# The state-space branch first: its projection leads, its steps stand between units of the attention projection, its lift stands ahead of attention

## The chip, the cores and the metric

The kernel runs on one core of one Trainium2 chip. The metric is the device time of one execution in microseconds (us). TensorE is called PE in the profile, VectorE DVE, ScalarE ACT, GpSimd POOL, and SP is the engine that issues most of the DMA transfers.

## The reference

It is one inference step of a small trunk with DEPTH = 2 layers over T = 384 tokens (three tiles of 128: one of context, two of latent tokens), D_MODEL = 1024, all in float32. Cut to what matters, a layer is:

```python
shift1, scale1, gate1, shift2, scale2, gate2 = mod      # six vectors from silu(c) @ w_ada + b_ada
h = rmsnorm(x) * (1 + scale1) + shift1
a, b, c, d, gate = split(h @ w_in)
ya = dense_attention(rope(norm(a_q)), rope(norm(a_k)) + cache, a_v + cache)        # branch A
yb = window_attention(..., sink)                                                   # branch B
yc = ssd_mixer(c_z, c_xbc, c_dt, state)                                            # branch C, state space
yd = rmsnorm(diff_attention(...)) * (1 - lam_init)                                 # branch D
out = sum(sigmoid(gate[n]) * (y[n] @ w_br[n]) for n in branches) @ w_out
x = x + gate1 * out
h2 = rmsnorm(x) * (1 + scale2) + shift2
x = x + gate2 * experts(h2)                              # 16 experts, each takes its own best tokens

def ssd_mixer(z, xbc, dt_raw, h0):                       # both directions
    u = silu(conv5(xbc)); xs, B, C = split(u)
    dt = softplus(dt_raw + bias); la = -exp(a_log) * dt
    acs = cumsum(la)                                     # per tile of 128 tokens
    y = ((C B^T) * exp(acs_i - acs_j)) (xs*dt) + C h_in * exp(acs) + d_skip * xs
    h_next = exp(acs_end) * h_in + B^T (to_end * xs*dt)
    return rmsnorm(y * silu(z))
```

## The kernel before

There is no planner. Each of the five engines has its instruction list written out by hand, once per layer (a hardware loop over li), and semaphores join them. What orders the work around the change is this.

**The banks.** Most products of TensorE go through four PSUM banks in turn. `big_results` (L82) writes down their order and which engine takes each. `bank(name)` (L596) makes TensorE wait until the result four places earlier has been taken; `grab` and `gave` are the other side. An engine takes its results in the order of its own list, so a result can be held up by something unrelated ahead of it there. Banks 4 to 7 belong to the attention steps and to the SSD products.

**The weights.** SP loads the 32 weight pieces of the mixers in the order of the numbers AT_ADA to AT_LIFT (L29 to L32) into a ring of SLOTS = 4 slots. Piece j goes to slot j % 4, and its transfer is issued only when TensorE has freed the slot from piece j - 4. A piece of w_ada, of a gate or of w_out has half the rows of a 1024x1024 block, 2 MB; a lift is one piece of 1 MB. Every product of two halves needs pieces j and j + 1.

**TensorE's order in a layer.** rows(0), rows(1) (products of the conditioning vector with w_ada), columns(0), columns(1) (their transposition); transposes of x (`widths`); projections of A and B (six units, 3 tiles x 2), of D (dqk and dv by tile), of C (z by tile, xbc by group of channels); six units of gate 0 with transposes of A's and B's queries and keys (qkT) among them, then the cached keys (ckT), D's (dT, cdT). Then the attention loop: for i = 0, 1, 2 (branches A, B, D) 12 steps (h, t) in a pipeline of scores, weights (transposes of the probabilities) and weighted, and in each step half a unit of gate(i + 1). After i = 0 and i = 1 stands lift(i): transposes of the branch (boT), then six products with w_br (up), which VectorE merges into xn. BRANCH = (0, 1, 3, 2), so C is last. rows(2) stands at the end of i = 2.

**The state-space part** stands behind all of this: transposes of the convolved channels (uT), the running sums (cum), the initial state (h0T), rows(3), decays(0), lift(2) for D, then for each tile t the scores GT, decays(t + 1) and, behind a wait for the masked scores (`mt_ready`, given by L1742), the products with Mt, xdt and xde. Then rows(4), the carried terms yo, columns(3), lift(3) for C, columns(4). The transposes of the merged m (mT) wait for `merged` at 18. Behind them stand the gate rows (gb), the output projection (out), rows(5) and the router, and then the expert stage.

**The other engines.** VectorE does the head norms with rotary embedding (`head_norm`, first A and B, then D), then the convolution (L1588, L1590), then the steps of attention, then the SSD elementwise work (L1694 to L1785, with C's norm at L1780). ScalarE copies results out of the banks, squares for the norms, takes the roots (`root(n)`, which waits for VectorE's variance), exp, silu and the tanh of the gates (L1237). The lines 578 and 587 are the helpers through which all of TensorE's matmuls and transposes go, so groups are told apart by tiles and shapes. Every float32 product shows as two passes in the profile.

Of the kernel before, what the change touches and what calls it, by code (L numbers as in the profile page):

```python
# [13 lines left out]
P = 128  # L14
D = 1024
# [23 lines left out]
BRANCH = (0, 1, 3, 2)  # L39
# [42 lines left out]
def big_results():  # L82
# [6 lines left out]
    out += [(("ab", t, b), "act") for b in range(2) for t in range(NT)]  # L89
    for t in range(NT):  # L90
        out += [(("dqk", t), "act"), (("dv", t), "act")]
    out += [(("z", t), "act") for t in range(NT)]
    out += [(("xbc", g), "act") for g in range(4)]
    out += [(("g", 0, s // 2, s % 2), "act") for s in range(3)]
    for t in range(NT):
        out += [(("qkT", t, b), "act") for b in range(2)] + [(("g", 0, (t + 3) // 2, (t + 3) % 2), "act")]
    out += [(("ckT",), "act")] + [(("dT", t), "act") for t in range(NT)] + [(("cdT",), "act")]
    for i in range(4):
        if i < 3:
            out += [(("g", i + 1, t, h), "act") for t in range(NT) for h in range(2)]  # L100
        if i == 2:
            out += [(("row", 2, h), "act") for h in range(2)]
            out += [(("uT", t), "act") for t in range(NT)]
            out += [(("cum",), "dve"), (("h0T",), "act")]
            out += [(("row", 3, h), "act") for h in range(2)]
            out += [(("dec", 0, d), "act") for d in range(2)]
        if i == 3:
            for t in range(NT):
                out += [(("GT", t, 0), "dve"), (("GT", t, 1), "dve")]
                if t + 1 < NT:  # L110
                    out += [(("dec", t + 1, d), "act") for d in range(2)]
            out.append((("row", 4, 0), "act"))
            out += [(("yo", t, g), "dve") for t in (1, 2) for g in range(2)]
            out += [(("row", 4, 1), "act"), (("col", 3), "dve")]
        out += [(("boT", i, k), "dve") for k in range(2)]
        out += [(("up", i, t, h), "dve") for t in range(NT) for h in range(2)]
    out.append((("col", 4), "dve"))
# [23 lines left out]
def trunk_kernel(nc, x_prompt, x_sample, cvecT, rowp, colp, caches, b_ada, w_ada, w_in, w_br, w_out, w_router,  # L141
                 w_e1, w_e3, w_e2, consts, y_prompt, y_sample, o_ak, o_av, o_bk, o_bv, o_ssm, o_dk, o_dv):
    with ExitStack() as ctx:
# [63 lines left out]
        cacc = at(po, 4 * NU_CONV).rearrange("p (i n) -> p i n", i=4)  # L207

        so = [qko]

        def over(n):
            so[0] += n
            assert so[0] <= qkend
            return at(so[0] - n, n)

        xsB = over(NT * 384).rearrange("p (t n) -> p t n", t=NT)
        E = over(8 * P).rearrange("p (j l) -> p j l", j=8)
        Mt = over(8 * P).rearrange("p (j l) -> p j l", j=8)
        xdt = over(1024).rearrange("p (i d h n) -> p i d h n", i=2, d=2, h=4)
# [100 lines left out]
        kv_out = sem("kv_out")  # L320
        ssm_out = sem("ssm_out")
# [182 lines left out]
        def _(pool):  # L504
            def parameters(li, first=False):
                pool.dma_start(cp[:, :], colp[li, :, :]).then_inc(params_c, 16)
                if first:

                    pool.wait_ge(loaded[(AT_AB + 1) % SLOTS], 16 * ((AT_AB + 1) // SLOTS + 1))
                    pool.dma_start(cst[:, NCST0:NCST], consts[:, NCST0:NCST]).then_inc(in_cst, 16)  # L510
# [10 lines left out]
            def mixers(li):  # L521
                pool.memset(xbc[:, :, :], 0.0).then_inc(pads, 1)

                pool.wait_ge(ab_ready, 1)
# [5 lines left out]
                pool.wait_ge(d_ready, 1)  # L530
                pool.dma_start(o_dk[0, li].rearrange("s h m d -> s (h m d)"), DQ[:, 0, 256:512]).then_inc(kv_out, 16)
                pool.wait_ge(big_act, taken_by(("dv", 0))[1])
                pool.dma_start(o_dv[0, li].rearrange("s h d -> s (h d)"), vd[:, 0, :]).then_inc(kv_out, 16)
# [7 lines left out]

                pool.wait_ge(st0_taken, 1)
                for d in range(2):
                    for g in range(2):
                        pool.dma_start(o_ssm[0, li, d, 2 * g:2 * g + 2].rearrange("h p n -> (h p) n"),
                                       sst[:, 2 * d + g, :]).then_inc(ssm_out, 16)
                bias_row(1, 5)
                pool.wait_ge(kv_out, (li + 1) * 96)
# [24 lines left out]
        def _(pe):  # L573
# [37 lines left out]
            with pe.Fori(0, DEPTH) as li:  # L611
# [73 lines left out]
                need(AT_AB)  # L685
                need(AT_AB + 1)
                for br in range(2):
                    for t in range(NT):
                        tokens(bank(("ab", t, br))[:, :], t, AT_AB, slice(br * 512, br * 512 + 512), signal=big,
                               free=(br == 1 and t == NT - 1))  # L690
                need(AT_D)
                need(AT_D + 1)
                for t in range(NT):

                    tokens(bank(("dqk", t))[:, :], t, AT_D, slice(0, 512), signal=big)
                    tokens(bank(("dv", t))[:, 0:ND_ - 512], t, AT_D, slice(512, ND_), signal=big, free=t == NT - 1)
# [14 lines left out]
                owed.append(freed[(AT_C + 1) % SLOTS])  # L711

# [17 lines left out]
                for s in range(3):  # L730
                    gate0(s)


                pe.wait_ge(in_cst, 16)
                pe.wait_ge(params, (li + 1) * 48)
                pe.wait_ge(ab_ready, 1)
                for t in range(NT):
                    for br in range(2):
                        b = bank(("qkT", t, br))
                        for g in range(2):  # L740
                            turn(b[:, g * P:(g + 1) * P], AB[:, t, br, g * P:(g + 1) * P])
                        turn(b[:, 256:384], AB[:, t, br, 256:384], signal=big)
                    gate0(3 + t)
                b = bank(("ckT",))
                turn(b[:, 0:P], ch("ak"))
                turn(b[:, P:2 * P], ch("bk"), signal=big)
# [7 lines left out]
                turn(b[:, P:2 * P], ch("dk")[:, P:2 * P], signal=big)  # L754
                taken(("cdT",))

# [69 lines left out]
                def lift(i):  # L826
                    j = AT_LIFT[i]
                    if i < 2:
                        pe.wait_ge(o_ready, (i + 1) * NIT)
                    else:  # L830
                        pe.wait_ge(bo_ready, i - 1)
                    for c in range(2):
                        b = bank(("boT", i, c))
                        for t in range(NT):
                            turn(b[:, t * P:(t + 1) * P], bo[:, t, c * P:(c + 1) * P], signal=big if t == NT - 1 else None)
# [10 lines left out]
                scores(0, 0)  # L846
                for i in range(3):
# [16 lines left out]
                pe.wait_ge(conv_out, 4)  # L864
                for t in range(NT):
                    b = bank(("uT", t))
                    for g in range(3):
                        turn(b[:, g * P:(g + 1) * P], uT[:, g, t * P:(t + 1) * P], signal=big if g == 2 else None)

                pe.wait_ge(dt_done, 1)  # L870
                b = bank(("cum",))
                for t in range(NT):
                    o = t * 16
                    mm(b[:, o:o + 4], c_("upto"), la[:, t, 0:4])
                    mm(b[:, o + 4:o + 8], c_("from"), la[:, t, 4:8])
                    mm(b[:, o + 8:o + 16], c_("ones"), la[:, t, :], signal=big if t == NT - 1 else None)
                b = bank(("h0T",))
                for d in range(2):
                    turn(b[:, d * P:(d + 1) * P], ch("ssm")[:, d * P:(d + 1) * P], signal=big if d else None)
                for h in range(2):  # L880
                    rows(3, h)

                def tri(d):
                    return c_("upto") if d == 0 else c_("from")


                def decays(t):
                    for d in range(2):
                        b = bank(("dec", t, d))
                        for h in range(4):  # L890
                            mm(b[:, h * P:(h + 1) * P], la[:, t, 4 * d + h:4 * d + h + 1].broadcast_to([P, P]), tri(d),
                               start=h == 0, stop=False, skip_group_check=True)
                        mm(b[:, :], ident, rep(c_("negbelow" if d == 0 else "negabove"), 1, 4), start=False, stop=True,
                           signal=big, skip_group_check=True)

                decays(0)
                lift(2)
                taken(("uT", 2))
                for t in range(NT):
                    for g in range(2):  # L900
                        b = bank(("GT", t, g))
                        r = slice(g * HD, (g + 1) * HD)
                        mm(b[:, 0:P], uT[r, 2, t * P:(t + 1) * P], uT[r, 3, t * P:(t + 1) * P], signal=big)
                    if t + 1 < NT:
                        decays(t + 1)
# [1083 lines left out]
```

## Time and profile before

| what | value |
|---|---|
| time, median of 3 runs | 2061.29 us (2060.68 to 2061.43) |
| the profiled execution, its own time | 2063.47 us |
| its span, first to last instruction | 2061.3 us |
| PE busy | 1910.1 us, 93% of the span |
| DVE, ACT, POOL busy | 481.8, 356.2, 48.2 us |
| mean granted TensorE clock | 0.965 of full speed |
| DMA | 532.98 MB, mean 259 GB/s |

The span falls into mixers and experts, twice. The mixers of layer 0 reach from 41.9 us (first projection) to 493.2 us (start of the output projection) and further to the first expert at 576 us; layer 1 repeats this from 1062 us on. PE busy is not PE at its peak, and the clock that was granted has to be read beside it.

### The profile page before, as it was taken

How to read it: one execution, taken by the hardware profiler on the slowest of the kernel's cores; microseconds unless marked ns; L12 is line 12 of the kernel's file. 1: busy time of each engine (PE TensorE's matmuls, PEld its weight loads, DVE VectorE, ACT ScalarE, POOL GpSimd, SP SyncE). 2: the span in 40 equal slices, each digit the busy share in tenths (PEclk: the TensorE clock that was granted, in tenths of full speed). 3: DMA queues.
4: the chain of work that ended last, by engine and by line, in shares of the span. 5: the costliest groups of instructions: out<-in, count | busy, mean ns of one | idle time of the engine just before them, and what ended most of it. 6: DMA issues, size and time to landing. Idle time of an engine off the chain costs nothing. (4 is left out here: it accounts for less than half of the span.)

```text
span 2061.3 us, 19828 instructions
## 1 busy us (share of the span) xinstructions
PE 1910.1 (93%) x7810; PEld 882.6 (43%) x7810; DVE 481.8 (23%) x1254; ACT 356.2 (17%) x920; POOL 48.2 (2%) x88
## 2 busy tenths in 40 slices
PE   5999999999899999898879999999998999989987
PEld 2464444455443433333345544544555333334322
DVE  1033124453410100100120522253534001001002
ACT  2123222421210100100021231224113001001000
POOL 2100000000300000000000000000000000000000
PEclk8999999988899999999989999999898999999999
DMA  9141113244689999999951411134436899999996
GB/s 376 62 166 68 52 51 123 90 183 179 227 327 408 426 429 428 428 429 428 422 207 62 174 61 62 41 123 171 159 122 245 351 426 424 429 428 428 429 428 271
DMA packets 65413, 532.98 MB, mean 259 GB/s; under 512 B 6657, under 2 KB 6785, under 8 KB 41281
## 3 DMA queue, kind: packets, MB, share of 16 engines
q1 hardware_dynamic: 62256, 527.59, 62.5%
q0 software_dynamic: 3088, 4.47, 0.6%
q8 instruction: 44, 0.72, 0.1%
q14 instruction: 25, 0.20, 0.0%
HBM read 529.16 MB, written 2.88 MB: 258 GB/s over the span
## 5 line engine op out<-in xcount | busy, mean ns | idle before, releaser
L578 PE MATMUL bank<-ring,hT 128*128 128x512 f32 (+2 forms) x1440 | 598.5, 569 | 2.7 <-DVE hT L1472 2.7
L578 PE MATMUL bank<-ring,scr 128*64 128x512 f32 (+1 forms) x2176 | 528.9, 598 | 44.4 <-DMA ring<-in_w_e 27.0
L578 PE MATMUL bank<-scr 128*64 128x512 f32 (+6 forms) x2048 | 437.7, 520 | 7.9 <-DVE dsm L1742 4.7
L578 PEld LDWEIGHTS bank<-ring,hT 128*128 128x128 f32 x1440 | 268.7, 191 | 271.3 <-issue 265.2
L578 PEld LDWEIGHTS bank<-ring,scr 128*64 128x64 f32 (+1 forms) x2176 | 175.6, 142 | 368.6 <-issue 309.1
L578 PEld LDWEIGHTS bank<-scr 128*64 128x64 f32 (+3 forms) x2048 | 183.2, 164 | 260.3 <-issue 251.9
L1885 DVE TENSOR_TENSOR scr<-scr,bank 128x512 f32<-128x512 f32 x32 | 22.0, 687 | 641.7 <-ACT scr L1394 641.7
L587 PE MATMUL bank<-cst,scr 128*128 128x128 f32 (+1 forms) x530 | 94.5, 294 | 40.4 <-ACT scr L1396 24.9
L587 PEld LDWEIGHTS bank<-cst,scr 128*128 128x128 f32 (+1 forms) x530 | 63.0, 159 | 102.3 <-issue 76.1
L1394 ACT ACTIVATE scr<-bank 128x512 f32<-128x512 f32 x32 | 19.1, 597 | 481.7 <-PE bank L578 481.7
L578 PE MATMUL bank<-ring,csw 128*32 128x512 f32 x384 | 58.0, 747 | 31.7 <-DMA ring<-in_w_ada 19.4
L1629 DVE TENSOR_REDUCE st<-bank 128x1 f32<-128x384 f32 (+1 forms) x48 | 22.5, 469 | 200.7 <-PE bank L578 200.6
L1398 ACT ACTIVATE scr<-bank 128x512 f32<-128x512 f32 x32 | 19.1, 597 | 247.3 <-PE bank L578 247.3
L578 PE MATMUL bank<-scr,xn 128*128 128x192 f32 (+3 forms) x288 | 50.5, 335 | 4.8 <-DVE scr L1850 2.4
L1237 ACT ACTIVATE scr<-bank 128x512 f32<-128x512 f32 x48 | 28.6, 597 | 138.3 <-PE bank L578 138.3
L578 PEld LDWEIGHTS bank<-scr,xn 128*128 128x128 f32 x288 | 44.8, 220 | 9.2 <-ACT scr L1389 5.1
L1286 ACT ACTIVATE scr<-bank,st 128x384 f32<-128x384 f32 (+1 forms) x48 | 24.5, 510 | 136.4 <-DVE st L1637 81.7
L1887 DVE COPY scr<-bank 128x384 f32<-128x384 f32 x32 | 17.9, 558 | 107.1 <-PE bank L587 107.1
L578 PE MATMUL bank<-hT,ring 128*128 128x384 f32 x128 | 41.6, 486 | 0.0
L578 PEld LDWEIGHTS bank<-ring,csw 128*32 128x32 f32 x384 | 12.7, 129 | 67.2 <-issue 43.0
L1292 ACT ACTIVATE scr<-bank,st 128x384 f32<-128x384 f32 (+1 forms) x48 | 24.0, 505 | 76.5 <-DVE st L1639 76.5
L1396 ACT ACTIVATE scr<-bank 128x512 f32<-128x512 f32 x32 | 19.1, 597 | 88.6 <-PE bank L587 88.6
(210 smaller groups left out, 1074.8 us busy)
## 6 DMA issues: line engine op xcount, KB each, us to landing
ring<-in_w_e SPq DMA_DIRECT2D x124, 2048.0 KB, 19.0
scr<-in_w_e SPq DMA_DIRECT2D x64, 2048.0 KB, 17.8
ring<-in_w_ada SPq DMA_DIRECT2D x24, 2048.0 KB, 9.9
ring<-in_w_in SPq DMA_DIRECT2D x20, 2048.0 KB, 8.0
ring<-in_w_br SPq DMA_DIRECT2D x8, 1024.0 KB, 7.2
ring<-in_w_out SPq DMA_DIRECT2D x4, 2048.0 KB, 8.6
ring<-in_w_in SPq DMA_DIRECT2D x4, 1552.0 KB, 16.3
ring<-in_w_in SPq DMA_DIRECT2D x4, 1536.0 KB, 6.7
```

Source lines behind the costliest of these rows:

```text
L578: ins = pe.matmul(out, lhsT, rhs, start=start, stop=stop, **kw)
L587: ins = pe.transpose(out, in_, ident[0:k, 0:k])
L1237: gave(("g", i, t, h), A(G[i % 2][:, t, h * HALF:(h + 1) * HALF], b[:, :], ACT.Tanh, scale=0.5))
L1286: ins = A(pr[:, n % 2, 0:nk], banks[4 + n % 2][:, 0:nk], ACT.Exp, bias=st[:, 1, q:q + 1], scale=HD ** -0.5, accum_out=st[:, 2, q:q + 1])
L1292: ins = A(pr[:, n % 2, m * T:m * T + nk], banks[4 + m][:, 0:nk], ACT.Exp, bias=st[:, 1, q + m:q + m + 1], scale=32 ** -0.5, accum_out=st[: ...
L1394: A(hs, banks[6][:, :], ACT.Silu).then_inc(silu_ready, 1)
L1396: A(hidT[:, :, :], banks[6][:, :].rearrange("p (b n) -> p b n", b=4), ACT.Copy).then_inc(hts_ready, 1)
L1398: A(yo, banks[7][:, :], ACT.Copy).then_inc(yo_ready, 1)
L1629: link(V.tensor_reduce(mx[:, 0:1], banks[4 + n % 2][:, 0:nk], AX.X, ALU.max))
L1885: V.tensor_tensor(hid.rearrange("p n b -> p (n b)"), hs, banks[7][:, :], ALU.mult).then_inc(hid_ready, 1)
L1887: V.tensor_copy(sgT.rearrange("p t c -> p (t c)"), banks[6][:, 0:T]).then_inc(sgs_ready, 1)
```

## The change

The order of branches is C, A, B, D. C is projected first (z, xbc), then D's dqk; dv stands behind the transposes uT. cum and h0T follow. The six units of the A/B projection alternate with decays, scores and products of the SSD steps; the carried terms follow the last unit. Of gate 0 two units stand ahead of the transposes of D and of the cached keys, three between them and the transposes of A's and B's queries and keys, one behind these. lift(0), now C's, stands between the first scores and the attention loop; lift(1) and lift(2) (A, B) stand where lift(0) and lift(1) stood, and lift(3) is D's. rows(3), rows(4), columns(3) and columns(4) follow the loop directly, ahead of lift(3). On VectorE the convolution, the SSD steps and C's norm move ahead of the head norm of A and B. On ScalarE C's squares and root(3) stand between two tanhs, and the squares of A and B and root(36) ahead of the evictions of D's transposes. E has two buffers; E, Mt and xdt lie in xn, the rest in the second gate buffer; C's result has a buffer of its own (boC). POOL stores D's keys and values and the final states ahead of A's and B's.

```diff
-AT_ADA = (0, 2, 20, 22, 25, 30)
-AT_AB, AT_D, AT_C, AT_OUT = 4, 6, 8, 28
-AT_GATE = (10, 12, 15, 18)
-AT_LIFT = (14, 17, 24, 27)
+AT_ADA = (0, 2, 21, 23, 25, 30)
+AT_C, AT_D, AT_AB, AT_OUT = 4, 6, 8, 28
+AT_GATE = (10, 13, 16, 19)
+AT_LIFT = (12, 15, 18, 27)
-BRANCH = (0, 1, 3, 2)
+BRANCH = (2, 0, 1, 3)
+AB_UNITS = [(t, b) for b in range(2) for t in range(NT)]
...
     out += [(("z", t), "act") for t in range(NT)]
     out += [(("xbc", g), "act") for g in range(4)]
+    out += [(("dqk", t), "act") for t in range(NT)]
+    out += [(("uT", t), "act") for t in range(NT)]
+    out += [(("dv", t), "act") for t in range(NT)]
+    out += [(("cum",), "dve"), (("h0T",), "act")]
...
+    out += [(("yo", t, g), "dve") for t in (1, 2) for g in range(2)]
+    out += [(("g", 0, s // 2, s % 2), "act") for s in range(2)]
+    out += [(("dT", t), "act") for t in range(NT)] + [(("cdT",), "act"), (("ckT",), "act")]
+    out += [(("g", 0, s // 2, s % 2), "act") for s in range(2, 5)]
+    out += [(("qkT", t, b), "act") for t in range(NT) for b in range(2)]
+    out += [(("g", 0, 2, 1), "act")]
...
         if i == 3:
+            out += [(("row", v, h), "act") for v in (2, 3, 4) for h in range(2)]
+            out += [(("col", 3), "dve"), (("col", 4), "dve")]
...
@@ TensorE @@
+                ab_unit(0)
+                decays(0)
+                ab_unit(1)
+                state_scores(0)
+                decays(1)
+                ab_unit(2)
+                state_products(0)
+                state_scores(1)
+                decays(2)
+                ab_unit(3)
+                state_products(1)
+                state_scores(2)
+                ab_unit(4)
+                state_products(2)
+                ab_unit(5)
+                pe.wait_ge(h_in, 1)
+                carried(1)
+                carried(2)
...
                 scores(0, 0)
+                lift(0)
                 for i in range(3):
...
                     if i < 2:
                         scores(i + 1, 0)
-                        lift(i)
+                        lift(i + 1)
+                for v in (3, 4):
+                    for h in range(2):
+                        rows(v, h)
                 columns(3)
+                columns(4)
                 lift(3)
-                columns(4)
...
@@ ScalarE @@
+                gate(0, 0)
+                for t in range(NT):
+                    act.wait_ge(u_ready, t + 1)
+                    A(Mt.rearrange("p j l -> p (j l)")[:, 256 * t:256 * (t + 1)], boC[:, t, :], ACT.Square,
+                      accum_out=st[:, 5, t:t + 1]).then_inc(act_sq, 1)
+                root(NT)
+                gate(0, 1)
+                act.wait_ge(d_ready, 1)
+                act.wait_ge(big_act, taken_by(("ab", NT - 1, 1))[1])
+                for t in range(NT):
+                    if t >= 2:
+                        act.wait_ge(sq_free, NT + t - 1)
+                    A(tmp[:, t % 2, :], AB[:, t, :, :].rearrange("p b n -> p (b n)"), ACT.Square).then_inc(act_sq, 1)
+                root(36)
+                for t in range(NT):
+                    b = grab(("dT", t))
+                    if t == 0:
+                        act.wait_ge(mt_ready, 2)
+                    A(dqT[:, :, t * P:(t + 1) * P], b[:, 0:256].rearrange("p (g t) -> p g t", g=2), ACT.Copy)
+                    gave(("dT", t), A(dkT[:, :, t * P:(t + 1) * P], b[:, 256:512].rearrange("p (g t) -> p g t", g=2), ACT.Copy))
```

## Rows read from the trace of the kernel before

**Rows 1.** Busy time by stretch, expert stage of layer 0: engines, granted clock, DMA share, GB/s

```profile
600.00:1000.00 400.00, 374.53 (x1751) 139.27 (x1748) 39.71 (x100) 32.35 (x59) 0.00 (x0) 1.00 1.00 423
```

**Rows 2.** Waits of TensorE, 40 to 495 us: releaser, us in total, times, longest

```profile
...
PE bank L578 <- DVE dsm L1742: 2.3, 1, 2.3
PE bank L587 <- DVE scr L1780: 2.2, 1, 2.2
...
PE bank L578 <- ACT scr L1265: 1.1, 1, 1.1
PE bank L587 <- ACT scr L1286: 0.6, 1, 0.6
PE bank L578 <- issue: 0.6, 1, 0.6
```

**Rows 3.** Timeline of TensorE, layer 0: start, us, operation, passes, wait before

```profile
188.83 1.47 PE L587 MATMUL bank<-cst,scr 128*128 128x128 f32 x12
...
406.20 1.92 PE L578 MATMUL bank<-ring,csw 128*32 128x512 f32 x16
...
412.07 5.05 PE L578 MATMUL bank<-ring,csw 128*32 128x512 f32 x32 [0.63 <-issue]
...
459.60 3.89 PE L578 MATMUL bank<-cst,scr 128*128 128x2 f32 x16
...
467.85 13.11 PE L578 MATMUL bank<-ring,scr 128*128 128x512 f32 x24 [0.65 <-DVE scr L1603]
480.79 3.66 PE L578 MATMUL bank<-cst,scr 128*128 128x2 f32 x16
484.32 5.36 PE L587 MATMUL bank<-cst,xn 128*128 128x128 f32 x24
...
539.89 3.23 PE L587 MATMUL bank<-cst,xn 128*128 128x128 f32 x24 [1.75 <-DVE xn L1462]
```

**Rows 4.** Busy time by stretch, at the lower clock: columns as in rows 1

```profile
483.20:490.50 7.30, 7.30 (x32) 6.80 (x33) 2.58 (x6) 1.96 (x4) 0.00 (x0) 0.53 1.05 436
462.90:473.10 10.20, 7.39 (x16) 3.86 (x17) 4.68 (x13) 0.38 (x2) 0.00 (x0) 0.50 0.79 321
449.40:456.00 6.60, 6.60 (x34) 4.09 (x32) 1.77 (x6) 0.00 (x0) 0.00 (x0) 0.51 0.00 0
411.80:415.00 3.20, 2.93 (x16) 0.91 (x20) 1.55 (x6) 0.12 (x1) 0.00 (x0) 0.50 1.03 413
193.40:196.70 3.30, 3.25 (x5) 1.63 (x6) 0.22 (x2) 0.84 (x3) 0.00 (x0) 0.53 0.72 297
```

**Rows 5.** Timeline of ScalarE: squares of A and B; tanh; a copy of dT

```profile
83.96 1.58 ACT L1195 ACTIVATE scr<-scr 128x768 f32<-128x768 f32 x2
...
188.81 0.60 ACT L1237 ACTIVATE scr<-bank 128x512 f32<-128x512 f32 x1 [1.89 <-PE bank L578]
...
189.84 0.40 ACT L1263 ACTIVATE scr<-bank 128x256 f32<-128x256 f32 x1
```

**Rows 6.** Timeline of VectorE: variance of A and B; SSD step 1

```profile
87.75 0.18 DVE L1443 TENSOR_SCALAR st<-st 128x36 f32<-128x36 f32 x1
...
439.79 0.42 DVE L1758 TENSOR_TENSOR scr<-scr,bank 128x256 f32<-128x256 f32 x1 [3.22 <-PE bank L578]
440.25 0.69 DVE L1716 TENSOR_TENSOR scr<-scr 128x512 f32<-128x512 f32 x1
440.86 1.28 DVE L1738 TENSOR_TENSOR scr<-scr,bank 128x512 f32<-128x512 f32 x2
```

**Rows 7.** Two loads of w_ada on SP's queue, each with its landing

```profile
L414 SPq DMA_DIRECT2D ring<-in_w_ada x1: 367/367/367, 404.6 to 404.6; - x1
...
DMA to landing us min/median/max: 7.4/7.4/7.4
...
L414 SPq DMA_DIRECT2D ring<-in_w_ada x1: 367/367/367, 416.3 to 416.3; - x1
...
DMA to landing us min/median/max: 9.9/9.9/9.9
```

More of the change, by code:

```diff
@@ L540, in mixers @@
                 bias_row(0, 2)
[L542 to L546, printed above, removed]
                 bias_row(1, 5)
-                pool.wait_ge(kv_out, (li + 1) * 96)
+                pool.wait_ge(kv_out, (li + 1) * 64)
+                pool.sem_inc(dummy, 1)
+                pool.wait_ge(d_out, (li + 1) * 32)
                 pool.sem_inc(dummy, 1)
@@ new lines, in _ @@
+                for t in range(NT):
+                    tokens(bank(("dv", t))[:, 0:ND_ - 512], t, AT_D, slice(512, ND_), signal=big, free=t == NT - 1)
+                pe.wait_ge(dt_done, 1)
+                b = bank(("cum",))
+                for t in range(NT):
+                    o = t * 16
+                    mm(b[:, o:o + 4], c_("upto"), la[:, t, 0:4])
+                    mm(b[:, o + 4:o + 8], c_("from"), la[:, t, 4:8])
+                    mm(b[:, o + 8:o + 16], c_("ones"), la[:, t, :], signal=big if t == NT - 1 else None)
@@ new lines, in _, with ab_unit @@
+                b = bank(("h0T",))
+                for d in range(2):
+                    turn(b[:, d * P:(d + 1) * P], ch("ssm")[:, d * P:(d + 1) * P], signal=big if d else None)
+                def ab_unit(n):
+                    t, br = AB_UNITS[n]
+                    if n == 0:
+                        need(AT_AB)
+                        need(AT_AB + 1)
+                    tokens(bank(("ab", t, br))[:, :], t, AT_AB, slice(br * 512, br * 512 + 512), signal=big,
+                           free=n == len(AB_UNITS) - 1)
@@ new lines, in tri, with decays @@
+                def tri(d):
+                    return c_("upto") if d == 0 else c_("from")
+                def decays(t):
+                    for d in range(2):
+                        b = bank(("dec", t, d))
+                        for h in range(4):
+                            mm(b[:, h * P:(h + 1) * P], la[:, t, 4 * d + h:4 * d + h + 1].broadcast_to([P, P]), tri(d),
+                               start=h == 0, stop=False, skip_group_check=True)
+                        mm(b[:, :], ident, rep(c_("negbelow" if d == 0 else "negabove"), 1, 4), start=False, stop=True,
+                           signal=big, skip_group_check=True)
@@ L728, in gate0 @@
                         gate(0, s, part)
[L730 to L746, printed above, removed]
+                gate0(0)
+                gate0(1)
                 pe.wait_ge(d_ready, 1)
@@ L877, in _ @@
[L877 to L894, printed above, removed]
@@ new lines, in decay @@
+                def decay(t):
+                    if t == 2:
+                        act.wait_ge(mt_ready, 1)
+                    for d in range(2):
+                        b = grab(("dec", t, d))
+                        for h in range(4):
+                            ins = A(E[t % 2][:, 4 * d + h, :], b[:, h * P:(h + 1) * P], ACT.Exp,
+                                    bias=nacs[:, t, 4 * d + h:4 * d + h + 1])
+                        gave(("dec", t, d), ins)
+                root(48)
+                ab_unit(0)
@@ new lines, in _ @@
+                sqs[0] += NT
+                dve.wait_ge(act_sq, sqs[0])
+                dve.wait_ge(u_ready, NT)
+                y = rsqrt(st[:, 5, 0:NT], NT, 256)
+                for t in range(NT):
+                    ins = V.scalar_tensor_tensor(boC[:, t, :], boC[:, t, :], y[:, t:t + 1], r_("gssm"), ALU.mult, ALU.mult)
+                    if t == NT - 1:
+                        ins.then_inc(bo_ready, 1)
+                    else:
+                        step(ins)
+                settle()
@@ L1775, in _ @@
[L1775 to L1785 removed]
+                        lift(i + 1)
```

557 lines of the change are left out of this document (260 added, 297 removed).

## The prediction

> **What bounds the kernel now.** I read the busy times by stretch first. In the expert stage the DMA engines are full, 423 GB/s from 600 to 1000 us [rows 1]; that stream starts on the progress of TensorE behind the mixers, so the stage keeps its length and only shifts. The mixers are the other way round. From 41.9 us (first projection of layer 0) to 493.2 us (first output projection) TensorE almost never stops; the waits that it has, apart from those of the lifts and of the step to branch D, which both kernels have, are in [rows 2], a few us a layer. Everything that the diff touches lies in this stretch, once per layer, so the price is: work of TensorE + its waits + what it loses to a lower clock, times two.
>
> The work is the same in both: the same matmuls and transposes, in another order. So I compare losses. The timeline [rows 3] and the granted clock [rows 4] show the second kind: in five stretches of 3.2 to 10.2 us the clock is at 0.50 to 0.55, the lower of the two levels (1.2 GHz for 2.4), and half of such a stretch is lost. Times below are those of layer 0.
>
> **What the change takes away, per layer.**
> - a. The entry to attention: waits of 1.1 and 0.6 us for the last transposed keys and the first exp [rows 2], then 3.3 us at half clock [rows 4]. The lift of C now stands there and covers them: 1.7 + 1.65 = 3.4.
> - b. The wait of 0.6 before rows(3) [rows 2] and 3.2 us at half clock [rows 4]: 0.6 + 1.6 = 2.2. (Its successor is g.)
> - c. The wait of 2.3 for Mt in the third SSD step [rows 2] and 6.6 us at half clock [rows 4]: 2.3 + 3.3 = 5.6. In the new place units of the A/B projection, 16 passes of 512 columns each, stand between the steps.
> - d. The wait of 2.2 for C's norm (L1780) [rows 2]: 2.2. C's norm is now needed only after six gate units.
> - e. columns(4), 16 passes 2 columns wide, moves from behind lift(3) to ahead of it. The transposes of m then come after a lift at full clock: 24 of them take 5.36 now, 3.23 in the same form later [rows 3]: 2.1.
>
> Sum 15.5 us.
>
> **What it adds, per layer.**
> - f. A wait at the cached-key transposes. ScalarE's order is now gate(0,1), three squares of AB, root(36), and only then the evictions of dT. The bank of ckT is that of dT 0, four results earlier. After the gate unit ends, ScalarE needs 0.6 for the tanh, then squares and VectorE's sums take from 83.96 to 87.93, 4.0 [rows 5, 6], then the root and two copies of 0.4 that overlap [rows 5], some 0.9: 5.5. TensorE has only 12 transposes, 1.47 [rows 3], and two more, 1.7 in all. It waits 3.8, and 0.2 for the next bank. Behind the waiting instruction stand gate units 2 to 4, which would have been ready. A clock loss like a's follows: 4.0 + 1.65 = 5.7. Bounds: 4.0 to 7.4.
> - g. rows(3) needs the second half of its weights, whose slot is freed by the last gate unit of the loop, which ends at 403.5. Its place in the queue is that of the load issued at 404.6 with 7.4 to landing: 412.0 [rows 7]. Now four us of state-space work (transposes, cum, h0T) stand between rows(2), which ends at 408.1 [rows 3], and rows(3); they are gone. Wait 4.0 plus b's clock loss of 1.6: 5.6. Bounds 4.0 to 7.4.
> - h. rows(4) follows at once, where SSD steps and a lift now give its loads more than 20 us. Its two loads wait for slots that rows(2) frees, are issued some 4 and 5 us after 403.5, and stand in the queue behind g's: 4.19 MB more. At 413 GB/s [rows 4] that is 10.2 us behind 412.0; by the landing at 426.2 of the load issued at 416.3, when 5.24 MB had followed in 14.2 us [rows 7], it is 11.4. I take 422.7. rows(3) runs from 412.0 for 5.1 [rows 3], to 417.1. Wait 5.6 plus clock 1.6: 7.2. Bounds 5.0 to 9.6.
> - i. The transposes of m wait for the last merge: two VectorE operations over 512 columns (L1616, L1618), 0.69 each like that at 440.25 [rows 6], 1.6 with latency. Today columns(4), 3.66 [rows 3], covers this. 1.6 (bounds 1.4 to 3.2).
> - j. The two columns stand back to back, 7.5 us with almost no columns streamed; the clock falls in them. The one measured partly at half clock took 3.89 beside 3.66 [rows 3]. 0.6 (0 to 2). lift(3) runs partly at half clock in both: 13.1 for 24 passes [rows 3].
>
> Sum 20.7 us. The nine transposes, cum (3 us of small passes, 0 to 1.6 of clock) and the SSD in front I put at nothing: what covers them is the projection. The load order costs nothing elsewhere, since use and queue have the same order in both; projecting C first (1.5 MB halves instead of 2) only makes the first weights earlier, and VectorE's hT, not the load, releases TensorE there. The stores of o_ssm and o_dk move forward on POOL's queue, are 32 to 128 KB, and no stage waits for them within tens of us.
>
> Net 20.7 - 15.5 = +5.2 per layer, +10.4 in two. The profiled span is 2061.3 (2063.5 with what lies around it), the median 2061.29, so the same base: **2071.7 us**.
>
> One rule of the Trainium skill differs from a row here. In "DMA: Bandwidth & Descriptors", section "Where 436 GB/s comes from", the HBM side binds a load at about 358 GB/s per core. The trace does not agree: 413 in the tail, 423 in the expert stage. By the rule h's loads would take 11.7 instead of some 10.7, 2 us more in two layers: 2073.7.
>
> **The rivals.**
> - R1, the columns do not drop the clock, so lift(3) runs at full speed. That saves half of 10.2 us less its idle part, some 3.3, and j: 3.9 a layer: 2071.7 - 7.8 = 2063.9, no measurable change. For it: at 412 to 473 each fall also had a real wait near. Against: from 483.2 to 490.5 TensorE was busy all of 7.30 us at 0.53 [rows 4], with only columns(4) ahead of it. The Trainium skill ("TensorE: Matmul & The Clock Gate", Part 1: The HAM clock gate) has the clock fall after an idle stretch, which here would mean R1; this last row speaks against that reading.
> - R2, the other side: g and h vanish, because the ada loads land ahead. Price 12.8 a layer: 2071.7 - 25.6 = 2046, faster. It decides from 7.2 of the 12.8 on. For it: DMA is idle through most of the attention. Against: four slots, and each load waits for the slot of four loads earlier, whose last reader is the last gate unit or rows(2) itself.
> - R3, the SSD steps stall in front too. Least slack: after the products of step 0 VectorE adds (0.42), decays (0.69) and multiplies (0.64, half of 1.28) [rows 6], 1.9 with latencies, before the bank of the next A/B unit is free. TensorE has 24 passes of scores and decays meanwhile, which take longer than the 3.23 of 24 transposes [rows 3]: over 1.3 of slack. The convolution and norm D have more. If this fails by 2 us in two steps, or by 2 us with a clock loss like a's, some 3.7 a layer: 2079.
> - R4, f does not come (5.7 a layer): 2060.3, the same. Nothing in the order of the program speaks for it.
>
> **How the numbers follow.** A measurement of this kernel tells some 0.2% from no change, 4.1 us. Forecast 0.50, R1 0.13, R2 0.12, R3 0.17, R4 0.08. Slower by over 0.2% (above 2065.4): the forecast nearly all (0.48) and R3: 0.65. Within: R1, R4, the rest of the forecast, less their spill: 0.20. Faster: R2 and spill: 0.15. The forecast's own bounds: all low ends give 14.4 - 15.5 = -1.1 a layer, 2059; all high ends, the 1.6 of cum with them, 31.2 - 15.5 = +15.7, 2093, but hardly all at once: 2064 to 2082. The range reaches down to take in R1 and R4 and leaves R2 out: 2058 to 2084.
>
> **What would show it.** In the profile after: no wait at Mt in the third step and no half clock near it (c); a wait of about 4 us for ScalarE's dT evictions ahead of the cached keys (f); waits of about 4 and 5.6 us on ring loads of in_w_ada in a place where none over 1 us is now (g, h); a wait of 1.6 on xn ahead of the transposes of m (i), whose 24 take 3.2; attention entered without a wait. Wrong would be: f's evictions early, rows(4) starting less than 14 us after the last gate unit, or waits between the A/B units.

## The result, and the profile of the changed kernel

The changed kernel takes 2069.2 us (median of 6 runs, 2067.3 to 2072.3) beside 2061.4 for the kernel before: a ratio of 1.0039, 95% interval 1.0026 to 1.0052. It is slower by some 8 us. One run of the kernel before took 2546 us, and the ratio leaves it out. The forecast of 2071.7 stands, and so does its sign.

Layer 0 of the profiled execution, span 2066.8 us. First the waits of TensorE from 40 to 500 us (releaser, us in total, times, longest); they answer to [rows 2].

```profile
PE bank L587 <- DMA ring<-in_w_ada: 9.0, 2, 4.9
PE bank L596 <- ACT scr L1319: 3.9, 1, 3.9
PE bank L587 <- DVE scr L1731: 3.5, 4, 1.1
PE bank L596 <- DVE scr L1791: 1.6, 1, 1.6
PE bank L596 <- DVE xn L1744: 1.5, 1, 1.5
...
```

The waits at Mt, for C's norm, at the entry to attention and before rows(3) are gone. In their place stand one for ScalarE's copies of dT (L1319), two for loads of w_ada and one for the last merge (L1744). The other two rows belong to both kernels. Now the timeline of TensorE that answers to [rows 3]:

```profile
183.22 0.38 PE L596 MATMUL bank<-cst,ca 128*128 128x128 f32 x2
187.52 0.44 PE L596 MATMUL bank<-cst,ca 128*128 128x128 f32 x2 [3.92 <-ACT scr L1319]
...
443.53 1.92 PE L587 MATMUL bank<-ring,csw 128*32 128x512 f32 x16
...
446.20 1.92 PE L587 MATMUL bank<-ring,csw 128*32 128x512 f32 x16
453.04 6.15 PE L587 MATMUL bank<-ring,csw 128*32 128x512 f32 x32 [4.91 <-DMA ring<-in_w_ada]
463.24 6.17 PE L587 MATMUL bank<-ring,csw 128*32 128x512 f32 x32 [4.05 <-DMA ring<-in_w_ada]
469.34 7.63 PE L587 MATMUL bank<-cst,scr 128*128 128x2 f32 x32
...
479.00 12.06 PE L587 MATMUL bank<-ring,scr 128*128 128x512 f32 x24 [0.65 <-DVE scr L1731]
492.57 2.84 PE L596 MATMUL bank<-cst,xn 128*128 128x128 f32 x24 [1.51 <-DVE xn L1744]
```

From 443.53 on: rows(2) in two halves, rows(3) behind a wait of 4.91, rows(4) behind one of 4.05 (it starts 19.7 us after the gate units end), both columns, lift(3), the transposes of m. And the stretches at the lower clock, columns as in [rows 4], with the whole mixers of the layer as the last row:

```profile
188.20:191.60 3.40, 3.40 (x5) 1.51 (x6) 3.33 (x5) 2.20 (x5) 0.00 (x0) 0.54 0.00 0
382.60:386.60 4.00, 3.63 (x6) 1.62 (x7) 2.56 (x8) 1.40 (x5) 0.00 (x0) 0.57 0.95 347
451.60:458.10 6.50, 5.06 (x24) 1.19 (x28) 0.00 (x0) 0.60 (x1) 0.00 (x0) 0.50 1.03 393
461.70:468.40 6.70, 5.16 (x28) 1.23 (x32) 0.00 (x0) 0.60 (x1) 0.00 (x0) 0.50 0.73 259
471.90:482.10 10.20, 9.55 (x32) 7.57 (x33) 1.64 (x5) 0.00 (x0) 0.00 (x0) 0.50 1.03 414
40.10:498.70 458.60, 438.90 (x1548) 228.39 (x1549) 152.42 (x406) 113.89 (x337) 19.45 (x35) 0.97 0.29 109
```

The mixers take 458.6 us. In the kernel before they took 451.3, with this row of its own:

```profile
41.90:493.20 451.30, 439.26 (x1547) 232.55 (x1548) 153.54 (x406) 112.82 (x336) 20.85 (x37) 0.97 0.30 115
```

The second number is TensorE's busy time: idle time went from 12.0 to 19.7, up 7.7; busy time hardly moved (439.3 to 438.9). So the layer paid in waits, and won next to nothing from the clock. Layer 1 says the same: its mixers went from 451.8 to 457.6.

### The profile page after: what moved, and what is told of

It is laid out like the page before. It is cut to its first block and busy times, and to the rows that moved or that the text cites. A ratio compares the mean times of both kernels' runs of the same rounds, so it can differ in the third digit from the quotient of the medians.

```text
span 2066.8 us, 19836 instructions
## 1 busy us (share of the span) xinstructions
PE 1902.0 (92%) x7810; PEld 868.5 (42%) x7810; DVE 480.5 (23%) x1254; ACT 359.5 (17%) x922; POOL 48.2 (2%) x88
## 5 line engine op out<-in xcount | busy, mean ns | idle before, releaser
L587 PE MATMUL bank<-scr 128*64 128x512 f32 (+7 forms) x1952 | 423.9, 530 | 0.9 <-ACT scr L1434 0.9
L587 PEld LDWEIGHTS bank<-scr 128*64 128x64 f32 (+3 forms) x1952 | 169.3, 160 | 254.8 <-issue 254.3
```

What stands on the lines that cost most here:

```text
L587: ins = pe.matmul(out, lhsT, rhs, start=start, stop=stop, **kw)
```

## The experiments

All are edits of the changed kernel, each timed beside the kernel before. Medians in us, ratio to the kernel before with its 95% interval:

| run | edit | median | ratio |
|---|---|---|---|
| x1 | copies of dT first on ScalarE | 2059.6 | 1.0002 (0.9989 to 1.0015) |
| x2 | lift(3) between rows(3) and rows(4) | 2054.2 | 0.9975 (0.9963 to 0.9987) |
| x3 | rows(2) ahead of lift(2) | 2059.5 | 1.0003 (0.9991 to 1.0016) |
| x4 | columns(4) behind lift(3) | 2067.6 | 1.0043 (1.0026 to 1.0060) |
| x5 | half of the bytes of rows(3), (4) left out | 2061.3 | 1.0004 (0.9994 to 1.0015) |
| x6 | SSD steps behind all A/B units | 2085.3 | 1.0125 (1.0105 to 1.0145) |
| x8 | x2 and x3 | 2051.0 | 0.9952 (0.9937 to 0.9967) |
| x7 | x1, x2 and x3 | 2036.0 | 0.9890 (0.9873 to 0.9908) |
| x9 | x7, columns inside the output projection | 2030.5 | 0.9851 (0.9835 to 0.9868) |
| x10 | only the columns inside the output projection | 2063.8 | 1.0012 (1.0000 to 1.0025) |
| x0 | none | 2074.0 | 1.0071 (1.0057 to 1.0085) |

The ratios tell each kernel from the kernel before. What an edit is worth beside the changed kernel is less sure: that kernel itself gave 1.0039 on one chip and 1.0071 on another, 7 us apart. So the times decide only where they differ by more, or where two runs share a chip (x1 to x4, x5 to x8, x10 and x0); the single steps are read from the traces.

**x1, step f.** On ScalarE:

```
 gate(0, 1)
 act.wait_ge(d_ready, 1)
+for t in range(NT):  # dT, then cdT and ckT
+    b = grab(("dT", t))
...
 for t in range(NT):
     A(tmp[:, t % 2, :], AB[:, t, :, :]..., ACT.Square)
 root(36)
-for t in range(NT):
-    b = grab(("dT", t))
...
```

> ScalarE evicts dT, cdT and ckT directly behind tanh(0,1), ahead of the squares and the root of the attention norm. Nothing else moves. Theory (step f of the prediction: the wait of 3.9 at ckT and the half clock of 3.4 us behind it come from the squares and the root standing in front of the evictions): both go, 5.6 us a layer, so 11 us in all and a time near 2058 us (2056 to 2061). Rival A: what is late is what the evictions need themselves, not their place; then they wait as long and the time stays at 2069. Rival B: squares and root now end some 2.5 us later and TensorE waits at qkT behind gate unit 4 instead; the wait moves, with 0 to 3 us a layer gained and a new row there.

TensorE's timeline of x1 at the cached keys:

```profile
185.11 0.60 PE L596 MATMUL bank<-cst,ca 128*128 128x128 f32 x4
185.76 20.87 PE L587 MATMUL bank<-ring,hT 128*128 128x512 f32 x48
```

The wait is gone, none replaces it at qkT, and TensorE runs on at full clock. The output projection starts 5.6 us sooner (493.07 for 498.68), although the first projection of this execution began 1.9 later (41.94 for 40.05): the mixers took 451.1 and 450.8, 7.5 and 6.8 less. That is more than f; in layer 0 the half clock at the D step, worth 1.7, is absent too. The order on ScalarE was the whole cause of the wait. What stood in front of the copies is seen in ScalarE's timeline of the changed kernel; a table load of 1.28 is part of it:

```profile
182.60 1.57 ACT L1312 ACTIVATE scr<-scr 128x768 f32<-128x768 f32 x2
184.53 0.84 ACT L1312 ACTIVATE scr<-scr 128x768 f32<-128x768 f32 x1 [0.36 <-DVE st L1517]
185.39 1.28 ACT L1171 ACT_TABLE_LOAD   x1
186.69 0.23 ACT L1171 ACTIVATE st<-st 128x36 f32<-128x36 f32 x1
186.82 0.37 ACT L1318 ACTIVATE scr<-bank 128x256 f32<-128x256 f32 x1
```

**x2, steps h, i and e.** On TensorE, and alike in the order of results and on the other engines:

```
-AT_ADA = (0, 2, 21, 23, 25, 30)
+AT_ADA = (0, 2, 21, 23, 26, 30)
-AT_LIFT = (12, 15, 18, 27)
+AT_LIFT = (12, 15, 18, 25)
...
 rows(3, h)
+lift(3)
 rows(4, h)
 columns(3)
 columns(4)
-lift(3)
```

> The state-space-independent lift(3) stands between rows(3) and rows(4), and columns(3) and (4) behind rows(4); the ring's order follows (lift piece 25, rows(4) pieces 26 and 27). Theory (step h: rows(4) waits because nothing but rows(3) lies between the end of the gate units and the landing of its second half; step i: mT waits for the last merge): both waits, 4.05 and 1.5, and the clock loss of 1.6 behind the first go; the two columns steps now stand right ahead of mT, whose 24 transposes fall back to half clock (2.8 to 5.4 us). Net 4.7 us a layer gained, near 2060 us (2056 to 2064). Rival A: the transfers are simply that long; the wait moves to lift(3)'s piece or to the output projection's pieces and little is gained (2066 to 2070). Rival B: columns do not lower the clock; mT keeps 2.8 and the time is near 2055.

Its timeline:

```profile
452.41 5.19 PE L587 MATMUL bank<-ring,csw 128*32 128x512 f32 x32 [4.55 <-DMA ring<-in_w_ada]
...
459.19 10.57 PE L587 MATMUL bank<-ring,scr 128*128 128x512 f32 x24 [0.79 <-DVE scr L1732]
469.69 3.64 PE L587 MATMUL bank<-ring,csw 128*32 128x512 f32 x32
473.26 7.63 PE L587 MATMUL bank<-cst,scr 128*128 128x2 f32 x32
480.75 5.36 PE L596 MATMUL bank<-cst,xn 128*128 128x128 f32 x24
```

rows(4) starts without a wait and takes 3.64 instead of 6.17; mT has no wait either, but takes 5.36. The stretches from lift(3) on, the columns from 473.3 to 480.9 in two parts:

```profile
459.20:473.30 14.10, 14.10 (x57) 5.46 (x57) 8.28 (x12) 0.60 (x1) 0.00 (x0) 1.00 0.98 375
473.30:476.10 2.80, 2.80 (x17) 2.80 (x13) 0.00 (x0) 0.60 (x1) 0.00 (x0) 0.99 1.02 392
476.20:480.90 4.70, 4.70 (x22) 4.70 (x22) 0.17 (x1) 0.00 (x0) 0.00 (x0) 0.50 1.02 417
480.90:486.00 5.10, 5.10 (x25) 5.10 (x26) 2.02 (x5) 1.96 (x4) 0.00 (x0) 0.50 1.03 413
```

TensorE is busy for all of the 12.7 us behind 473.3, and for 14.1 us ahead of them it had no wait at all; still the clock falls within the columns. That decides against R1: it falls without a wait while these matmuls, two columns wide, run. The time, 2054.2, is below the range that I gave (2056 to 2064) and is that of rival B, but rival B's sign, mT at 2.8, did not come. The mixers gained 10.8 and 7.6, not 4.7: the rest is clock, since rows(3), rows(4), lift(3) and its six transposes all ran shorter (5.19, 3.64, 10.57 and 0.87 for 6.15, 6.17, 12.06 and 1.52), and the half clock at the D step was absent in layer 0.

**x3, steps g and h.** rows(2) and its pieces ahead of lift(2):

```
-AT_ADA = (0, 2, 21, 23, 25, 30)
+AT_ADA = (0, 2, 18, 23, 25, 30)
-AT_GATE = (10, 13, 16, 19)
+AT_GATE = (10, 13, 16, 21)
-AT_LIFT = (12, 15, 18, 27)
+AT_LIFT = (12, 15, 20, 27)
...
 if i == 2 and n >= NIT:
-    rows(2, n - NIT)
+    rows(3, n - NIT)
 if i < 2:
     scores(i + 1, 0)
+    if i == 1:
+        for h in range(2):
+            rows(2, h)
     lift(i + 1)
```

> rows(2) and its two pieces stand ahead of lift(2), in the middle of attention; rows(3) takes its place in the last two gate slots, with pieces that are asked for long before. Rows(4), columns and lift(3) follow as in the changed kernel. Theory (steps g and h are one shortage: four pieces asked for in the last 20 us): the wait of 4.9 at rows(3) and its clock loss of 1.6 go; rows(4) still waits about 4 and loses 1.6, because its pieces are asked for only when the last gate units free their slots. 6.5 us a layer gained, near 2056 us (2053 to 2060). Rival A: the wait at rows(4) grows by what rows(3) loses, the sum stays, 2066 to 2070. Rival B: rows(2) in the middle waits itself for its pieces, or delays the first scores of the third branch, and 2 us or more of the gain are given back there.

One wait on w_ada is left (4.32 ahead of rows(4)); rows(2) brings none in the middle. The mixers took 452.6 and 451.5, 6.0 and 6.1 less, near the 6.5 expected. The median fell by less than the 13 us that two layers should give, but ended inside the range.

**x4, steps e and j.**

```
 columns(3)
-columns(4)
 lift(3)
+columns(4)
```

> columns(4) goes back behind lift(3), as in the kernel before; all else as changed. Theory (steps e, i, j): mT's wait of 1.5 for the last merge goes, since columns(4) covers it; mT stands right behind columns(4) at half clock again, 5.4 instead of 2.8 us; columns(3) alone is at full clock when it starts. Net +0 to +1 us a layer: 2068 to 2072. Rival (the columns do not lower the clock): mT keeps 2.8 and the wait goes, so 1.5 us a layer or more gained, near 2066.

```profile
484.87 3.66 PE L588 MATMUL bank<-cst,scr 128*128 128x2 f32 x16
488.39 4.27 PE L597 MATMUL bank<-cst,xn 128*128 128x128 f32 x24
```

mT's wait is gone and its 24 transposes take 4.27 instead of 2.84: i is taken away and e comes back, in part (5.4 was expected), and the median is 1.7 below the changed kernel's and just below the range given, too little to tell from it. The columns cost 3.89 and 3.66 apart and 7.63 together, so j is 0.1.

**x5, what g and h wait for.**

```
 for v in range(6):
-    plan[AT_ADA[v] + h] = (w_ada[li, rows, v * D:(v + 1) * D], D, 4)
+    n = HALF if v in (3, 4) else D
+    plan[AT_ADA[v] + h] = (w_ada[li, rows, v * D:v * D + n], n, 4)
...
-cols = slice(h * HALF, (h + 1) * HALF)
+cols = slice(0, HALF) if v in (3, 4) else slice(h * HALF, (h + 1) * HALF)
```

Half of these two weight matrices is left out; both halves of each product come from the same 512 columns.

> The pieces of rows(3) and rows(4) are loaded with 512 of their 1024 columns, and both halves of each are computed from these 512; so half of these two weight matrices is left out. The count of instructions on TensorE is the same. Theory (steps g and h: the waits are the bytes of four pieces at some 420 GB/s, asked for too late): the wait of 4.9 at rows(3) falls to 2 to 3, the one of 4.05 at rows(4) goes with its clock loss of 1.6. 8 us a layer, near 2053 us (2048 to 2060). Rival: a transfer's fixed time from issue to landing, not its bytes, makes the wait; then the waits stay within 1 us of 4.9 and 4.05, and the time stays above 2064.

```profile
452.83 3.64 PE L588 MATMUL bank<-ring,csw 128*32 128x512 f32 x32 [1.63 <-DMA ring<-in_w_ada]
459.12 3.64 PE L588 MATMUL bank<-ring,csw 128*32 128x512 f32 x32 [2.64 <-DMA ring<-in_w_ada]
```

With half the bytes the waits go from 4.91 and 4.05 to 1.63 and 2.64, and the clock no longer falls behind them: both rows take 3.64. So bytes make about half of the waits (9.0 to 4.3 in all). I had expected the second to vanish, and the time at 2053 (2048 to 2060); it came out at 2061.3, outside. Why the second stays is seen on SP's queue: the last load of rows(4) is issued at 453.9, only 1.1 us after rows(3) starts, and lands 5.2 later, when rows(4) starts (the section on the prediction says what holds its issue back). The mixers gained 9.1 and 7.2, about as reckoned. In the profiled execution the stretches outside the mixers took 9.5 us more than in that of the changed kernel; x0 below shows how far these move by themselves.

**x6, step c.** All six `ab_unit` ahead of the first `decays`, on TensorE, on ScalarE and in the order of results:

```
-ab_unit(0)
-decays(0)
-ab_unit(1)
...
+for n in range(len(AB_UNITS)):
+    ab_unit(n)
+decays(0)
+state_scores(0)
+decays(1)
+state_products(0)
...
```

> All six A/B units first and only then the three state-space steps, one behind the other, on TensorE and ScalarE alike; the rest as in the changed kernel. Theory (steps b and c: what took the waits at Mt and the half clock near them away is that the steps stand between A/B units): each step now waits for decay exponentials on ScalarE and for Mt on VectorE, with nothing to cover it. At least the 2.3 at Mt and half clock around it come back, 5 to 12 us a layer more, 2079 to 2093 us, near 2085. Rival: what took them away is only that the state-space branch comes before attention, wherever its steps stand; then no wait at Mt and 2067 to 2071 us.

```profile
PE bank L583 <- DVE dsm L1667: 2.3, 1, 2.3
...
PE bank L583 <- DVE dsm L1685: 0.8, 1, 0.8
```

```profile
168.00:179.00 11.00, 9.09 (x40) 7.00 (x41) 6.11 (x18) 0.00 (x0) 0.00 (x0) 0.53 0.01 1
```

The wait of 2.3 at Mt is back to the tenth, one of 0.8 at VectorE's L1685 with it, and 11.0 us at 0.53. The median is the 2085 expected. What took c away is that the steps stand between the units, not that the branch comes first.

**x8 and x7, the tail and then the head as well.** x8 joins x2's edit and x3's; x7 adds x1's.

> The edits of the two runs before together: rows(2) ahead of lift(2), rows(3) in the last two gate slots, lift(3) between rows(3) and rows(4), columns(3) and (4) ahead of mT. Theory (each took away one of the two ring waits, and they are independent here, because pieces are asked for a lift earlier): no wait on w_ada is left, mT has no wait and stands at half clock (5.4). Beside the run with lift(3) between (2054.2): 4.6 of wait and about 1.6 of clock less a layer, so near 2042 us (2038 to 2047). Rival A: lift(3) comes so early that it waits for VectorE's norm of the third branch, 2 to 5 us a layer: 2047 to 2052. Rival B: the output projection's second piece, whose slot lift(3) frees, lands late: a new wait there.

> The run with rows(2) early and lift(3) between, and the evictions of dT, cdT and ckT ahead of the squares and the root as well. Theory: the three losses that the change added are separate; beside the kernel with both tail edits 4 to 5.6 us a layer less (the wait of 3.9 gone, the clock stretch of 3.4 us at half rate too), so near 2033 us (2028 to 2040), faster than both kernels. Rival: the gain of one is partly taken back by another wait, for example at the norm of attention or at the end of C; then 2040 to 2046.

TensorE's timeline of x7 behind the last rows(3):

```profile
446.47 1.28 PE L598 MATMUL bank<-cst,scr 128*128 128x128 f32 x6 [2.77 <-DVE scr L1820]
448.40 13.14 PE L589 MATMUL bank<-ring,scr 128*128 128x512 f32 x24 [0.65 <-DVE scr L1738]
461.47 3.64 PE L589 MATMUL bank<-ring,csw 128*32 128x512 f32 x32
465.04 7.63 PE L589 MATMUL bank<-cst,scr 128*128 128x2 f32 x32
472.53 5.24 PE L598 MATMUL bank<-cst,xn 128*128 128x128 f32 x24
```

No load of w_ada is waited for. Rival A of x8 holds: lift(3) now comes so early that it waits 2.8 for the norm of branch D (L1820), in x8 as in x7, and the lift behind it takes 13.1 (13.5 in x8) instead of x2's 10.6, at a lower clock. Hence 2051.0 and not 2042. It is a wait of the same kind as that of [rows 2] which step d took away, but for another norm: there C's, here D's, which rows(3), rows(4) and the columns cover in the changed kernel.

x7 is 15 us below x8, on the same chip, where f is worth 11. In layer 0 the difference shows in the clock. In x7 it never falls from 42 to 446 us; in x8 it falls behind f's wait for 6.9 us, and again at 388:

```profile
42.00:446.00 404.00, 397.16 (x1412) 205.60 (x1410) 139.84 (x385) 108.33 (x327) 17.25 (x31) 1.00 0.26 95
```

```profile
186.90:193.80 6.90, 5.44 (x8) 2.48 (x9) 6.28 (x15) 4.33 (x11) 0.00 (x0) 0.52 0.00 0
388.20:391.90 3.70, 3.70 (x6) 1.56 (x6) 2.25 (x7) 1.40 (x5) 0.00 (x0) 0.54 0.98 385
```

**x9 and x10, the columns.** Within each of the first two units of the output projection, in place of `columns(3)` and `columns(4)`:

```
for k in range(KD):
    tokens(b[:, :], t, AT_OUT, slice(h * HALF, (h + 1) * HALF), signal=big, ks=range(k, k + 1))
    mm(bc[:, 2 * k:2 * k + 2], quads(rsb[:, v % 2, :], k), c_("sel"),
       signal=big if k == KD - 1 else None)
```

> As the kernel with all three edits (2036.0), but columns(3) and columns(4) stand inside the first two units of the output projection: behind each of the eight passes over the contraction one pair of columns. Their 32 matmuls stay. Theory (what lowers the clock is a stretch of 7.6 us of matmuls two columns wide, although TensorE is busy all through it, and mT pays 2.5 us a layer because it stands behind it): mixed with matmuls 512 columns wide the columns leave the clock at full, mT falls from 5.3 to 2.9 us, and the columns cost 7.6 us or less. 2.5 to 5 us a layer less, 2026 to 2031 us. Rival A: the clock falls for another reason (the waits before it, or the count of instructions), mT stays at 5.3, and the time is 2034 to 2038. Rival B: the columns' row of the next norm is now late; a wait behind the output projection takes the gain back.

> The changed kernel with one edit: columns(3) and columns(4) stand inside the first two units of the output projection, as in the run before; lift(3) follows rows(4) directly. Theory (the prediction's forecast against its rival R1: it is the columns themselves that lower the clock ahead of lift(3)): the half clock behind rows(4) ends sooner, the 24 passes of lift(3) fall from 12.06 to about 10.6 us and its six transposes from 1.5 to 0.9, and the columns cost 6.4 us instead of 7.6. 3 us a layer less than the changed kernel, near 2063 us (2060 to 2066). R1: the clock was low only from the wait at rows(4); the lift, now right behind it, is slower than before or as slow, and only the 1.2 a layer of the columns is gained, 2066 to 2068. Other rival: lift(3)'s own piece is not there yet; a wait of 1 us or more at in_w_br.

In x9 the transposes of m, and the output projection with the columns in it:

```profile
469.57 2.84 PE L599 MATMUL bank<-cst,xn 128*128 128x128 f32 x24
```

```profile
475.70:494.80 19.10, 19.10 (x65) 13.32 (x64) 1.52 (x4) 0.60 (x1) 0.00 (x0) 1.00 0.98 403
```

The same 32 narrow passes, mixed with wide ones, leave the clock at 1.00, and mT falls from 5.24 to 2.84. In x10, without the rest of the edits, the lift answers as expected:

```profile
467.46 10.57 PE L587 MATMUL bank<-ring,scr 128*128 128x512 f32 x24 [0.79 <-DVE scr L1738]
```

12.06 became 10.57, and the whole is 10.2 us below x0 on the same chip, where some 6 were expected. x9 at 2030.5 is the fastest of all, 1.5% below the kernel before. That it is 5.5 below x7 rests on different chips, and its profile bears out less: mixers and router together, which share the columns' time between them, took 1.1 us a layer less than in x7, in x9's slowest run (2035.1).

**x0, the changed kernel again.**

> The changed kernel once more, with no edit, beside the run above on the same chip: what one profiled execution of it tells from another. Theory (the clock falls of the prologue and the router depend on how they lie against it, not on the mixers): the waits inside the mixers repeat within 0.5 us each (3.9, about 4.9 and 4.05, 1.6, 1.5), the two mixers within 2 us of 458.6 and 457.6, while the first projection starts anywhere from 39.8 to 42.7 us; median 2066 to 2072. Rival: the waits move from execution to execution by more than 1 us, and the comparison by single profiles above is worth less.

```profile
PE bank L587 <- DMA ring<-in_w_ada: 9.1, 2, 4.7
PE bank L596 <- ACT scr L1319: 3.9, 1, 3.9
...
```

The waits inside the mixers repeat within 0.7 us each (0.5 was expected), and the mixers, at 459.5 and 456.5 us, within 1.2. Yet this chip gave 2074.0 and a ratio of 1.0071, outside the first interval and above the 2072 expected. The profiled spans are 2071.5 and 2066.8; the difference lies outside the mixers. Mostly it is the router of layer 1 (84.8 for 80.5 us from the first output projection to the first expert); the start of the first projection adds 1.2 (41.21 for 40.05).

## Why the prediction came out right

Step by step, layer 0, in us:

| step | predicted | measured | by |
|---|---|---|---|
| a, b, d | -7.8 | -7.8 | their waits and half clock are absent; D's norm is waited for instead in x7, 2.8 |
| c | -5.6 | -5.6 | absent; back in x6 |
| e | -2.1 | -2.5 | mT 2.84 for 5.36 |
| f | 5.7 | 5.5 | 3.92, and 0.46 of 3.4 us |
| g | 5.6 | 7.4 | 4.91, and rows(3) at 6.15 for 3.64 |
| h | 7.2 | 6.6 | 4.05, and rows(4) at 6.17 for 3.64 |
| i | 1.6 | 1.5 | 1.51 |
| j | 0.6 | 0.1 | 7.63 for 3.89 + 3.66 |
| not foreseen | 0 | 1.7 | 0.43 of the 4.0 us at 382.6, in layer 0 alone |
| net | +5.2 | +6.9 | mixers measured: +7.3, in layer 1 +5.9 |

Every wait and every fall that the forecast named was there, in its place. The table does not close, though: lift(3) took 12.06 for 13.11, which I had put at no change. With it the terms give 5.9, and 1.4 of the 7.3 that the mixers of layer 0 lost has no term.

The waits alone were forecast at +8.4 (4.0 + 4.0 + 5.6 + 1.6, less 6.8 of the old ones) and came to +7.7. The error is in the clock, which I had giving back 3.2 a layer; it gave back 0.4. Two terms were mis-sized. The losses behind g and h were put at 1.6 each, after b's; but rows(3) and rows(4), right behind a wait of over 4 us, ran for 5.1 and 5.2 us at half clock and took 6.2 instead of 3.6: 2.5 each. And I costed no fall behind waits that both kernels have: the wait of 1.6 at the D step had none in the kernel before, and had one in the changed kernel, at 382.6. The two waits, 4.9 and 4.05, were forecast at 4.0 and 5.6; their sum, 9.0, at 9.6.

In h one reading failed, and it was luck that it cost nothing. I had both loads of rows(4) issued some 4 and 5 us after the gate units end. The first was (447.3, behind 443.53). The second was issued 11.5 us behind them:

```profile
L420 SPq DMA_DIRECT2D ring<-in_w_ada x1: 368/368/368, 455.0 to 455.0; - x1
...
DMA to landing us min/median/max: 8.2/8.2/8.2
```

Its slot is released by the first matmul behind rows(2) that has no signal of its own to give, and in the new order that is the first of rows(3), which was itself waiting for its weights. The loads ahead of it filled the time: the second half for rows(3) and the two for rows(4) landed at 453.0, 458.1 and 463.2, 5.1 us apart. 2.10 MB in 5.1 us is 411 GB/s, the rate of the forecast, so by this estimate the load would have landed no sooner if it had been issued in time. rows(4) started 19.7 us behind the gate units, 19.2 by the forecast. In x5, with half the bytes, the late issue does show.

In j a row was misread. The columns that took 3.89 in the kernel before were not the ones more at half clock (the granted clock was 0.92 over them, 0.84 over those of 3.66); how long these columns take does not follow the clock at all, as the last section shows.

The mixers therefore cost 13.2 us in two layers, not 10.4. The span rose by only 5.5, because the other stretches were 7.7 shorter in this execution: the first projection began 1.8 sooner, the experts of layer 0 took 2.6 less, the router of layer 1 2.7 less. x0 shows such stretches moving by 5 us with no edit. So 2071.7 lies between the two measured medians, 2069.2 and 2074.0, partly by luck: two errors of opposite sign met.

The rivals. R1 is refuted by x2, and by x10, where lift(3) without the columns ahead of it ran at full clock: the columns do drop it. The Trainium skill ("TensorE: Matmul & The Clock Gate", Part 1: The HAM clock gate) ties the fall to an idle engine; by that rule alone the 12.7 us of x2 would have run at full clock, and the trace, with TensorE busy throughout, does not agree. R2 is refuted by the two ring waits; but x8 shows that both can be taken away by asking for the pieces sooner. R3 did not come: no wait stands between A/B units. R4 did not come by itself, and x1 shows that moving six lines would have brought it.

What stays open: the mixers of x3 and x5 took 12 and 16 us less in two layers, but their medians are only 9.8 and 7.9 us below the changed kernel's 2069.2. The comparisons are of different chips, and of mixers in single executions; that the stretches outside take the rest by clock falls that come and go fits x0, but was not shown for those runs.

## What to carry to other kernels

Before a stage is moved, list for each engine what its neighbours were covering: the change took away all that it was to take away (15.9 us a layer) and lost more, because the moved work had been hiding four loads and a merge, and because one engine's queue had root(36) ahead of copies that another waited for. Both are order, not work: x7 keeps the new front, orders the loads and the copies anew, and is 1.1% faster than the kernel before. The 32 narrow passes of this kernel belong between wide ones.

## What was not expected of the hardware

The price of a wait in clock is not fixed. Behind the same wait of 3.9 at the cached keys the clock was low for 3.4 us in the changed kernel, for 6.9 in x8. Behind the wait of 1.6 at the D step it stayed full in one kernel and fell in another.

How long the columns take did not follow the clock. In x2 the 32 passes of columns(3) and (4) start 0.23 us apart both at 0.99 and at 0.50, and they take 7.63 in all in every kernel where they stand together; what stands behind them pays for the fall, while TensorE shows busy all through. This holds for these columns only. columns(0) and (1), at the start of the layer, are just as many and as wide, and in the changed kernel they took half as long:

```profile
30.70 3.73 PE L587 MATMUL bank<-cst,scr 128*128 128x2 f32 x32
```

They start 0.11 apart at full clock, and 0.21 apart where the clock was low (layer 1 of the kernel before). In the program their matmuls differ in one thing: columns(3) and (4) read their 128x128 operand with a stride of four floats (`quads`), columns(0) and (1) without. That the stride makes the difference, and whether columns without it would lower the clock, was not tested.
